# Down projection as seven half-size products in place of one, with rows 512-1023 finished first

## The reference, cut to what matters

```python
SEQ = D_MODEL = 1024;  D_FF = 2816
f = rms_norm(x, pre_ffn_g[i])
f = (jax.nn.silu(f @ w_ffn_gate[i]) * (f @ w_ffn_up[i])) @ w_ffn_down[i]
x = x + rms_norm(f, post_ffn_g[i])

e = p[i] @ w_ple_up[i]
gate = jax.nn.sigmoid(x @ w_ple_gate[i])
x = x + rms_norm(gate * e, ple_norm_g[i])
```

## Time and profile before

| | |
|---|---|
| time, median of 3 runs | 1638.87 us (1638.39 to 1639.7) |
| span of the profiled execution | 1633.5 us |
| median less span (what lies around it) | 5.4 us |
| TensorE busy | 1547.8 us, 95% |
| DVE, ACT, POOL busy | 837.1, 521.7, 245.0 us |
| down projection | about 1260 to 1503.6 us of the span |
| first gate matmul of the last stage | 1512.04 us |

### The profile page before, as it was taken

The page is one execution under the profiler, slowest core; times in us unless marked ns, Lnnn a source line. Parts: engine busy times, 40 slices in busy tenths (PEclk is TensorE's granted clock), DMA queues, the critical chain, the costliest instruction groups (busy, mean ns, idle before and its releaser), DMA issues.

```text
span 1633.5 us, 19991 instructions
## 1 busy us (share of the span) xinstructions
PE 1547.8 (95%) x7448; PEld 1234.5 (76%) x7448; DVE 837.1 (51%) x1218; ACT 521.7 (32%) x1001; POOL 245.0 (15%) x368
## 2 busy tenths in 40 slices
PE   6999999987789899999999999999999999999997
PEld 5887788876655666656788888888888888887886
DVE  5658888986678999943321111111111335445553
ACT  5444433134543434344311110111111324433321
POOL 5444366238300000000000000000000000000000
PEclk9999999998999999999999999999999999999999
DMA  6222233252110000010321111111101111232110
GB/s 194 71 59 75 70 102 110 97 222 94 48 44 26 27 26 14 14 52 14 90 78 38 39 51 51 51 51 51 51 26 51 48 50 50 92 103 97 52 65 39
DMA packets 96481, 105.47 MB, mean 65 GB/s; under 512 B 7840, under 2 KB 72096, under 8 KB 96416
## 3 DMA queue, kind: packets, MB, share of 16 engines
q1 hardware_dynamic: 96416, 104.61, 20.7%
HBM read 85.72 MB, written 18.87 MB: 64 GB/s over the span
## 4 chain that ended last, share of the span: by engine, by line
PE 73%; DVE 10%; DVEq 6%; issue 5%; ACT 3%; POOL 3%; SPq 1%; DMA 0%; POOLq 0%; ACTq 0%
PE ps L528 20%; PE ps L530 20%; PE ps L529 20%; PE ps L754 4%; DVEq L1455 4%; DVE m L1452 3%; DVE lm L1544 2%; DVE sc L1441 2%; DVEq L1453 1%; PE ps L699 1%; PE ps L716 1%; PE ps L707 1%; ACT pt L1107 1%; PE ps L645 1%; PE ps L643 1%
## 5 line engine op out<-in xcount | busy, mean ns | idle before, releaser
L528 PE MATMUL ps<-fth,wh 128*128 128x512 f32 x704 | 274.5, 390 | 1.1 <-ACT ftr L1141 1.1
L529 PE MATMUL ps<-ftl,wh 128*128 128x512 f32 x704 | 274.0, 389 | 0.0
L530 PE MATMUL ps<-fth,wl 128*128 128x512 f32 x704 | 273.9, 389 | 0.0
L1603 DVE TENSOR_TENSOR ht<-sg,ps 128x512 f32 (+1 forms) x44 | 30.2, 687 | 366.8 <-ACT sg L1163 366.8
L1452 DVE MAX8 m<-sc 128x8 f32<-128x384 f32 (+5 forms) x192 | 171.1, 891 | 13.1 <-issue 2.9
L1454 DVE MATCH_REPLACE8 sc<-m,sc 128x384 f32<-128x384 f32 (+5 forms) x192 | 168.1, 876 | 0.3 <-issue 0.3
L528 PEld LDWEIGHTS ps<-fth,wh 128*128 128x128 f32 x704 | 132.1, 188 | 29.1 <-ACT ftr L1141 1.3
L1163 ACT ACTIVATE sg<-ps 128x512 f32<-128x512 f32 x44 | 26.3, 599 | 398.6 <-PE ps L530 398.6
L529 PEld LDWEIGHTS ps<-ftl,wh 128*128 128x128 f32 x704 | 132.1, 188 | 27.5 <-issue 0.2
L530 PEld LDWEIGHTS ps<-fth,wl 128*128 128x128 f32 x704 | 132.1, 188 | 27.5
L528 PE MATMUL ps<-dh,hth 128*128 128x512 f32 x352 | 137.3, 390 | 1.3 <-DVE htl L1658 1.3
(11 more groups left out here) (219 smaller groups left out, 2771.3 us busy)
## 6 DMA issues: line engine op xcount, KB each, us to landing
raw<-in_w_in SPq DMA_DIRECT2D x48, 256.0 KB, 3.1
dr<-in_w_ffn_down SPq DMA_DIRECT2D x44, 256.0 KB, 2.6
wr<-in_w_ffn_gate SPq DMA_DIRECT2D x21, 512.0 KB, 4.1
wr<-in_w_ffn_up SPq DMA_DIRECT2D x21, 512.0 KB, 5.3
ret_rows<-stg SPq DMA_DIRECT2D x32, 320.0 KB, 3.5
rp<-ret_rows SPq DMA_DIRECT2D x8, 1280.0 KB, 6.4
xn<-in_x SPq DMA_DIRECT2D x8, 512.0 KB, 5.2
wo<-in_w_out SPq DMA_DIRECT2D x1, 4096.0 KB, 20.1
```

The costliest lines, as they stand in the source:

```text
L528: pe.matmul(o, ah, wh, start=start, stop=False)
L529: pe.matmul(o, ah, wl, start=False, stop=False)
L530: return pe.matmul(o, al, wh, start=False, stop=stop)
```

## The change

The rows of `HT` are halved (0-511 and 512-1023), the 22 blocks are halved (0-10, `TOP`, and 11-21, `BOT`) and the output columns are halved. By Strassen's rule the eight half-size products are replaced by seven, made of sums of halves. They run in the order M5, M2, M3, M1, M6, M4, M7, 11 steps each, so 77 steps (n = 0 to 76) of 4 row tiles x 3 = 12 matmuls. In each step:

- the weights: two blocks are loaded and POOL adds or subtracts them (`dsum`), in all products but M5 and M2, which take one block;
- the hidden operand: two halves of `HT` are added or subtracted (`hsum`): by POOL in M5 and M2 and the odd steps of M7, by DVE in M1, M6 and the even steps of M7; M3 and M4 need none;
- ACT makes both high parts, DVE both low parts, all 512 wide. They have three buffers: the parts of step n can be made once step n-3 is done.

M3 goes on in the banks that hold M5, M6 in those of M1, M4 in those of M2; sums that are needed twice leave PSUM (`M25`, `M1D`). Rows 512-1023 are complete after M4, and rows 4 to 7 of the eight row tiles enter the last stage first; the new x of the first two and its transposes lie within M7. The embedding product of the first row tile comes behind its gate product. POOL also makes eight corrections (lines 1984 and 1989 of the kernel after).

The core of the diff:

```diff
+    FH = FT // 2
+    ROWS1, ROWS2 = slice(0, 512), slice(512, 1024)
+    TOP, BOT = 0, FH
+    A_TERMS = (((TOP, ROWS1), (BOT, ROWS1), ALU.add), ((TOP, ROWS2), (BOT, ROWS2), ALU.add), ((TOP, ROWS1),),
+               ((TOP, ROWS1), (BOT, ROWS2), ALU.add), ((TOP, ROWS2), (TOP, ROWS1), ALU.subtract), ((BOT, ROWS2),),
+               ((BOT, ROWS1), (BOT, ROWS2), ALU.subtract))
...
+    def hs_engine(n):
+
+        m, phi = divmod(n, FH)
+        if len(A_TERMS[m]) == 1:
+            return None
+        return "p_hs" if m in (M5, M2) or (m == M7 and phi % 2 == 1) else "v_hs"
...
+        for n in range(DSTEPS):
+            m, phi = divmod(n, FH)
             pe.wait_ge(s["v_dwl"], n + 1)
             pe.wait_ge(s["v_dhl"], n + 1)
...
+            for r in range(4):
+                if phi == 0:
+                    bank_free(m, r)
+                rs = slice(r * P, (r + 1) * P)
+                ends = phi == FH - 1
+                ins = mm3(bank(BANK0[m] + r), HTH[n % 3][:, rs], HTL[n % 3][:, rs], DH[n % 3][:, :], DL[n % 3][:, :],
+                          phi == 0 and OPENS[m], ends, not OPENS[m])
...
+            if n == 2:
+                embedding_transposes()
+            if n == 72:
+                x2_transposes(0)
+            if n == 75:
+                x2_transposes(1)
...
+        def hidden_sum(n):
+
+            m, phi = divmod(n, FH)
+            if hs_engine(n) != "v_hs":
+                return
+            dve.wait_ge(s["v_ht"], 2 * FT)
+            dve.wait_ge(s["t_dn"], n - 2)
+            (f0, r0), (f1, r1), op = A_TERMS[m]
+            v.tensor_tensor(HSUM[n % 3][:, :], HT[:, f0 + phi, r0], HT[:, f1 + phi, r1], op).then_inc(s["v_hs"], 1)
...
+            if n == product_end(M1) + 2:
+                dve.wait_ge(s["v_wgl"], 1)
+                for r in range(4):
+                    dve.wait_ge(s["t_acc"], acc_count(M1, r))
+                    dve.wait_ge(s["v_z"], r + 1)
+                    v.tensor_tensor(M1D[:, r, :], bank(r), M25[:, r, :], ALU.subtract).then_inc(s["v_z"], 1)
...
+            if len(B_TERMS[m]) == 3:
+                pool.wait_ge(load_dr[n % 2], raw_landed(n))
+                pool.wait_ge(s["t_dn"], n - 2)
+                g_.tensor_tensor(DSUM[n % 3][:, :], RAWD[n % 2][:, 0, :], RAWD[n % 2][:, 1, :], B_TERMS[m][2])\
+                  .then_inc(s["p_ds"], 1)
```

More of the change, by code:

```diff
@@ L194, in build @@
-    WGR = [sb(f"wgr{i}", [P, D], 192 + 8 * i) for i in range(2)]
+    RAWD = [sb(f"rawd{i}", [P, 2, 512], 2 + 4 * i) for i in range(2)]
+    DSUM = [sb(f"dsum{i}", [P, 512], a) for i, a in enumerate((176, 184, 192))]
+    DL = [sb(f"dl{i}", [P, 512], a, F32R) for i, a in enumerate((176, 184, 192))]
+    DH = [sb(f"dh{i}", [P, 512], a, F32R) for i, a in enumerate((178, 186, 194))]
+    HSUM = [sb(f"hsum{i}", [P, 512], a) for i, a in enumerate((172, 180, 188))]
+    HTL = [sb(f"htl{i}", [P, 512], a, F32R) for i, a in enumerate((172, 180, 188))]
@@ L342, in build, with store_out @@
+    for i in range(RT):
+        squares.append(("u", i))
     sq_at = {u: n + 1 for n, u in enumerate(squares)}
[L343 to L347, removed]
+    WG_LOAD_STEP = (50, 52, 54, 56, 70, 72, 74, 76)
+    WG_SPLIT_STEP = (54, 56, 58, 60, 73, 74, 76, 76)
+    WG_FREE_STEP = (47, 49, 51, 53, 67, 69, 71, 73)
     PROLOGUE = ((0, 0), (1, 0), (0, 1), (1, 1))
+    def store_out(sp, i):
+        r = ROWS_IN_TURN[i]
+        sp.wait_ge(s["v_out"], i + 1)
+        sp.dma_start(out[0, r * P:(r + 1) * P, :], UU[i % 2][:, :]).then_inc(st_out[i % 2], 16)
@@ L479, in _ @@
[L479 to L492, removed]
-                if t % 2 == 1:
-                    sp.wait_ge(s["v_wgl"], i * 2 + (t // 2 + 1))
-                    sp.dma_start(WGR[t // 2][:, :], w_ple_gate[0, bass.ds((i * 2 + t // 2) * P, P), :])\
-                      .then_inc(load_wg[t // 2], 16)
@@ L520, in _ @@
+        hidden_sums_done(DSTEPS - 1)
+        row_gain(GPL, ple_norm_g, "load_gain")
+        for i in range(RT):
+            if i + 2 < RT:
+                sp.wait_ge(s["v_x2"], i + 1)
+                load_x1(i + 2)
+            if i >= 2:
+                store_out(sp, i - 2)
+        for i in range(RT - 2, RT):
+            store_out(sp, i)
         for i in range(2):
@@ L935, in embed @@
             m.then_inc(s["t_em"], 1)
-        x2_transposes(0)
-        embed(0)
-        x2_transposes(1)
-        for r in range(RT):
-            gate(r)
-            if r:
-                embed(r)
-            if r + 2 < RT:
-                x2_transposes(r + 2)
+        for i in range(RT):
+            gate(i)
+            embed(i)
+            if i + 2 < RT:
+                x2_transposes(i + 2)
     @block.scalar
```

664 lines of the change are left out of this document (357 added, 307 removed).

## The result

The changed kernel takes 1645.97 us (median of 5 runs, 1644.85 to 1651.55), the kernel before 1639.21 (5 runs, 1638.39 to 1640.34). The ratio is 1.0049, 95% interval 1.0036 to 1.0063. It is slower by 7 to 8 us, where 5 us less was forecast. Its runs also scatter more than those of before.

A forecast was written before the change was run, and what follows sets the result against it. TensorE's matmuls were taken to bound the kernel. Gains of 34.7 us less 29.2 us of new waits made 5.5 us less, from 1638.9 to 1633.4, rounded to 1633.5 us; range 1624 to 1640, chance 0.48.

The forecast's parts named there:

- The start: Start of the down stage: TensorE waits 2.7 us for the first step's parts, made behind the hidden matrix's last half.
- the 0.8: Slow clock after the hole at the down stage's start: half of 1.6 us, taken as 0.8 us lost.
- The gains: Down stage and its end: fewer matmuls, less work behind the last one and less idle time, 34.7 us saved.
- The price of the shared resource: DVE and POOL passes over SBUF exclude each other: 0.55 us per DVE and 1.15 us per POOL instruction of 512 columns.
- The second rival: POOL's sum comes at the wrong place: M1 and M6 lose 26 us, M7 17 to 20; 1653.6 us, chance 0.24.
- The third rival: Weight loads set the pace, 18 or 9 us over M3 and M4; 1643 us at the latter; chance 0.11.
- the first: Rival in which the shared time hides, by overlap or lead, leaving the start and 0 to 5 us: 1610 us, chance 0.17.
- the term of waits in the products: New TensorE waits: 1 us in M5, M2, M3 and M4, 10.6 in M1 and M6, 13.7 in M7.
- the good case: M1 and M6: POOL's sum fits into DVE's wait for ACT, 2.95 us per step, 9.5 us lost.
- half-way case: M1 and M6 at 3.35 us per step, half way to the wrong place for POOL's sum: about 1646 us.
- Hidden; but extras fall into steps 4 to 6, so I count 1 us: M5, M2, M3, M4: shared time 2.25 us under 2.72 per step; embedding extras cost 1 us, bounds 0 and 5.
- the good place. I take 10.6 (3.0 per loop): M1 and M6: POOL asks 0.3 us into an hsum, so 3.0 us per loop and 10.6 us lost.

The follow-up runs named there:

- experiment 7: Changed kernel with POOL also making every hsum of M1 and M6 in place of DVE: 1655.96 us.
- experiment 3: Changed kernel loading only one weight block per step, POOL adding a block of the hidden matrix to it instead of the second block: 1647.28 us.
- experiments 4 and 5: Changed kernel with, first, POOL's sum in M1 and M6 waiting for DVE's hsum: 1648.33 us; second, M1's four evacuations one step earlier: 1645.76 us.
- dve_all: Changed kernel with all POOL's down-stage sums and corrections on DVE, first two steps' parts, embedding loads and split, and new x moved: 1622.78 us, ratio 0.99.

## Why the prediction was wrong, by its steps

**What held.** The matmuls (924, 0.227 apart). The start: 2.79 for 2.7, though no slow clock followed (M5's window is at 1.00), so the 0.8 was nothing. The end: gate product after 0.70. The gains were 36.3 us by the traces (before 243.3 + 8.7 + 109.3 to the last gate matmul; after, without any wait, 209.5 + 3.9 + 0.2 + 111.4), for 34.7. The price of the shared resource, 0.55 and 1.15 us, taken turn about: it is what late M6 and the 3.40 us of experiment 7 show, and the Trainium skill ("SBUF — State Buffer", "Who interferes with whom") has the same rule. The second rival's 3.7 us per step is the 3.73 of late M6. The third rival, transfers, is excluded by experiment 3, the first by the blocked instructions.

**What failed** is the term of waits in the products: 1 + 10.6 + 13.7 = 25.3 us, measured 40.8. In parts, transposes taken off: M5, M2, M3, M4 8.9 for 1; M1 and M6 16.6 for 10.6; M7 15.3 for 13.7. Rival 2 had the sign, but its waits were M1 and M6 with 26 and M7 with 18.5. M1 and M6 came to 16.6, since M1 ran at 2.91 a step, nearly the 2.95 of the good case, and 8.9 came from four products where it had next to none. That its half-way case says 1646 is luck.

The step that failed first is "Hidden; but extras fall into steps 4 to 6, so I count 1 us". For the bare loop it was right: most steps of M2, M3 and M4 take 2.72 us. But the extras were not all counted. Four of the eight splits of gate weights stand behind steps 54, 56, 58 and 60, DVE's evacuations (the copies or sums out of PSUM) of M2 and M6 behind the parts of steps 23 and 57, and ACT's of M5, M3 and M4 behind those of the second step of the next product; none of them is in the sum of any product. There the time went: TensorE had holes of 0.6, 1.3, 1.6 and 1.7 us at the ends of M5, M2, M3 and M4, and of 0.7 and 0.6 before steps 58 and 59. Timelines of DVE, ACT and PE at the end of M3, then DVE in M4:

```profile
1360.80 1.78 DVE L1704 TENSOR_TENSOR hsum<-ht 128x512 f32<-128x512 f32 x1
1363.71 2.04 ACT L1334 COPY fo<-ps 128x512 f32<-128x512 f32 x4
1364.43 0.47 PE L581 MATMUL ps<-dh,hth 128*128 128x512 f32 x1 [1.46 <-ACT fo L1334]
...
1446.55 2.47 DVE L1775 TENSOR_TENSOR fo<-ps,m 128x512 f32<-128x512 f32 x4
```

At the end of M3 an `hsum` is held up by POOL, ACT makes the high parts after it, and only then empties the bank for which TensorE waits. With the sums on DVE the hole there is 0.5. In M4 DVE takes 12.85 us (1440.81 to 1453.66) for the parts of steps 56 to 59 with two splits and four evacuations between them, and TensorE needs 10.9 for four steps.

The second step that failed is "the good place. I take 10.6 (3.0 per loop)". M1 found that place, late M6 did not: five of its steps took 3.73. That is 5 x 0.73 = 3.7 us, and 1.7 more is a slow clock in M6's first step; with these 10.6 becomes 16.0, of the 16.6 measured. That the order in which the engines ask decides between 2.91, 3.2 and 3.73 is what experiments 4 and 5 show.

The third step at fault is the clock, priced at 0.8 us for the start alone, with 1.6 us each only in a rival. It fell four times in the down stage, each time around a hole of TensorE; 34 matmuls came 0.43 apart, which is 34 x 0.2 = 6.8 us, and that is part of the excess above.

A sum over the whole stage from the same prices, POOL 90 x 1.15 + DVE 182 x 0.55 + 14 wide ones x 1.08 = 218.7 us against some 213 us of TensorE, says that not everything fits. But by itself it gives 6 us of loss, less than the 25.3 of the products taken singly, and with the sums on DVE it falls to 183 while 19.3 us of waits remain. That this total decides is not shown.

How much is sharing? Leaving out POOL's weight sums takes 24.5 us from the stage; moving 60 sums to DVE, where each holds the resource for 0.55 instead of 1.15, takes 21.4 us for 36 us less of shared time. Both include the clock that came back (the slow matmuls fell from 34 to 12 and 7, that is 4.4 and 5.4 us). In dve_all, where no POOL pass is left to share with, 18.2 of the 40.8 us of waits remain: 4.9 in M5 (the split of the embedding weights), 3.4 in M4, 6.1 in M7, 3.8 in the rest. So 22.6 us, a little over half, went when POOL's passes did; what the moved sums cost in DVE's queue is in this number and was not separated. M4's 3.4 have their holes at steps 58 and 59 as in after, so there the cause is DVE's own queue of splits and evacuations; M7's lie from step 72 on, around the new x and the gate weights. How much of those is DVE's wide instructions and how much the ACT chain was not separated.

## What to carry to other kernels

Before giving "idle" GpSimd some work beside a busy VectorE, add up both engines' exclusive time for each stretch, with every instruction that stands in it: the evacuations where a product ends and the wide splits too, not only the loop. Here the loops of four products had slack (2.25 us of 2.72), and the extras left out of the sum were part of 8.9 us lost where 1 was counted. Price a loop that is near full by its bad order as well; which order comes was not foreseen here (2.91 or 3.73 us a step for the same work). The same sum costs half the shared time on VectorE (0.55 against 1.15 us here), so moving work onto the engine that looks busier can be the cure: a ratio to before of 1.0049 became 0.9935 by that alone, and 0.9893 with the corrections and the start moved. If moving instructions about only moves the hole, take work away.

## What the runs showed of the hardware

The clock after a hole. Timeline of PE and windows of after, around the end of M1 (columns as in rows 3):

```profile
1399.85 0.59 PE L581 MATMUL ps<-dh,hth 128*128 128x512 f32 x1 [3.45 <-DVE m1d L1770]
```
```profile
1396.40:1399.80 3.40, 0.00 (x0) 0.00 (x0) 2.66 (x5) 1.14 (x2) 1.32 (x1) 1.00 0.59 202
1400.00:1403.40 3.40, 3.40 (x9) 2.65 (x9) 2.66 (x5) 1.14 (x2) 0.00 (x0) 0.51 0.60 233
```

TensorE stood still for 3.45 us at a granted 1.00, and as soon as it worked again the clock was 0.51 (1.2 GHz). A hole of 2.06 us before 1488.28 was also followed by a slow clock, while the one of 2.63 us at the start was not: the length of the hole alone doesn't tell.

GpSimd's sum of a tile with itself was quicker than that of two tiles (1231 against 1488 ns in the mean, blocked time included). And small instructions are blocked too: DVE's first 128x1 instruction for the new x, at 1488.15 in after, began while POOL's correction ran and took 1.23 us, the second, of another kind and on its own, 0.15. In dve_all, without a POOL pass beside it, that first instruction took 0.15 as well.
